# Expert rows two apart, and the experts' products in four column groups, in a two-block transformer with 64 routed experts

## What is computed

```python
# MOE_GROUPS = 8, MOE_PER_GROUP = 8 (64 experts), MOE_TOPK = 2, MOE_FF = 256, D_MODEL = 1024, 512 tokens
g_sel = jnp.argmax(g_logits, axis=-1)
e_prob = jax.nn.softmax(e_logits[tok, g_sel], axis=-1)
top_p, top_i = lax.top_k(e_prob, MOE_TOPK)
gates = g_w[:, None] * top_p / jnp.sum(top_p, axis=-1, keepdims=True)
expert_id = g_sel[:, None] * MOE_PER_GROUP + top_i
...
hid = jax.nn.silu(xb @ w1[e]) * (xb @ w3[e])
return hid @ w2[e]
...
out = jnp.zeros((n_tok + 1, dm), ys.dtype).at[slot_tok].add(ys)[:n_tok]
```

## Time and profile before

| | us |
|---|---|
| median of 3 runs | 1604.18 (1602.31 to 1608.41) |
| the profiled execution, its own time | 1606.86 |
| span of the profile | 1605.1 |
| PE busy in the span | 1407.7 (88%) |
| weight loads PEld | 995.9 (62%) |
| ACT busy | 491.7 (31%) |
| DVE busy | 417.4 (26%) |
| POOL busy | 629.1 (39%) |

### The profile page before, as it was taken

One profiled execution on the slowest core, in us unless ns is written; L12 is line 12 of the kernel. 1 busy time (PEld: TensorE's weight loads), 2 busy tenths in 40 slices (PEclk: granted clock), 3 DMA queues, 4 the chain that ended last, 5 costly groups with the idle time before them and its releaser, 6 DMA issues. The chain is left out here.

```text
span 1605.1 us, 22033 instructions
## 1 busy us (share of the span) xinstructions
PE 1407.7 (88%) x8290; PEld 995.9 (62%) x8290; DVE 417.4 (26%) x1057; ACT 491.7 (31%) x1083; POOL 629.1 (39%) x726
## 2 busy tenths in 40 slices
PE   7999999898999999998999978669988887888781
PEld 6688876676888888886677857434444444444440
DVE  3003047713111102212245041532211111111114
ACT  4326357733322222223464312212211111111111
POOL 4334545443444444443458433123332222222222
PEclk9999999998999999999899989779999999999996
DMA  3322311031332233321313314749999999999964
GB/s 126 119 97 101 109 38 42 29 105 53 105 105 79 79 105 106 105 79 54 118 53 106 105 32 186 301 166 392 393 400 403 407 402 397 391 386 392 389 265 161
DMA packets 91463, 300.17 MB, mean 187 GB/s; under 512 B 12980, under 2 KB 35664, under 8 KB 66816
## 3 DMA queue, kind: packets, MB, share of 16 engines
q1 hardware_dynamic: 83136, 283.37, 47.0%
q0 software_dynamic: 8160, 15.75, 2.8%
q10 hardware_dynamic: 96, 0.08, 0.0%
HBM read 294.94 MB, written 12.62 MB: 192 GB/s over the span
## 5 line engine op out<-in xcount | busy, mean ns | idle before, releaser
L471 POOL TENSOR_TENSOR wring_halves<-wring,wring_halves 128x512 fp32r<-128x512 f32 (+1 forms) x275 | 357.8, 1305 | 409.5 <-ACT wring_halves L466 408.8
L466 ACT CAST wring_halves<-wring 128x512 fp32r<-128x512 f32 (+1 forms) x275 | 168.4, 618 | 465.3 <-PE ps L1035 442.0
L1033 PE MATMUL ps<-wring_halves,big_halves 128*128 128x512 f32 x612 | 244.2, 399 | 16.9 <-POOL wring_halves L471 13.5
L1033 PE MATMUL ps<-hT_halves,wring_halves 128*128 128x512 f32 (+1 forms) x496 | 195.2, 393 | 5.0 <-DVE big_halves L1553 5.0
L1034 PE MATMUL ps<-big_halves,wring_halves 128*128 128x512 f32 (+1 forms) x496 | 194.8, 393 | 0.0
L1035 PE MATMUL ps<-hT_halves,wring_halves 128*128 128x512 f32 (+1 forms) x496 | 194.5, 392 | 0.0
L2209 POOL DMA_INDIRECT y_dram<-xn,sidx x64 | 57.1, 891 | 325.6 <-DVE xn L1969 283.6
L1034 PE MATMUL ps<-wring_halves,hT_halves 128*128 128x512 f32 x436 | 173.1, 397 | 0.0
L1035 PE MATMUL ps<-wring_halves,hT_halves 128*128 128x512 f32 x436 | 172.4, 395 | 0.0
L1460 PE MATMUL ps<-big,arena 128*32 128x256 f32 x1024 | 124.6, 395 | 36.7 <-DMA big<-in_moe_w_dram 36.2
L1033 PEld LDWEIGHTS ps<-wring_halves,big_halves 128*128 128x128 f32 x612 | 117.1, 191 | 45.3 <-POOL wring_halves L471 16.6
(11 more groups left out here) (328 smaller groups left out, 1833.0 us busy)
## 6 DMA issues: line engine op xcount, KB each, us to landing
big<-in_moe_w_dram SPq DMA_DIRECT2D x86, 1024.0 KB, 23.7
wring<-in_moe_w_dram SPq DMA_DIRECT2D x66, 1024.0 KB, 26.3
wring<-in_ffn_w_in_dram SPq DMA_DIRECT2D x22, 1024.0 KB, 6.6
hT<-in_moe_w_dram SPq DMA_DIRECT2D x20, 1024.0 KB, 22.9
wring<-in_fox_w_in_dram SPq DMA_DIRECT2D x7, 2048.0 KB, 8.2
wring<-in_gla_w_in_dram SPq DMA_DIRECT2D x6, 2048.0 KB, 7.9
mkv<-in_moe_w_dram SPq DMA_DIRECT2D x10, 1024.0 KB, 30.1
xn<-in_moe_w_dram SPq DMA_DIRECT2D x10, 1024.0 KB, 30.2
```

The lines of the kernel that those rows point to most:

```text
L466: act.copy(hi, src).then_inc(s_hi, 1)
L471: pool.tensor_tensor(lo, src, hi, ALU.subtract).then_inc(s_lo, 1)
L1033: pe.matmul(out, lhs[1], rhs[0], start=start, stop=False)
```

## The change

There are two parts.

**Places.** The index row `iow` used to hold 0, 1, 2, ..., 31. Now it holds 0, 16, 1, 17, 2, 18, ...: row 2s holds place s and row 2s+1 holds place 16+s. An expert with at most 16 tokens now has them in the even rows 0, 2, 4, ..., where it had them in rows 0 to 15. Gather, scatter and the order of the rows in all products follow the same table. Nothing else in them changes.

**Products.** gate_up makes four products of 128 columns for each k instead of two of 256, each into its own 32 rows of the bank: group i has half i // 2 of the hidden width and its even or odd elements. The gate part is then 128 rows by 64 columns, and so is the up part. The silu and the product take one instruction each instead of two. The two transposes become two ordinary products with the identity, each of 64 columns in its own 64 rows of one bank. expert_down makes four products of 256 columns for each k instead of two of 512. The copies to `ye` are two of 32x256 on each of ACT and DVE instead of one of 32x512.

```diff
-                act.activation(msg[j % 2][0:C, :], bank(2 + j % 2)[0:C, 0:P], ACT.Silu)
-                act.activation(msg[j % 2][G2:G2 + C, :], bank(2 + j % 2)[G2:G2 + C, 0:P], ACT.Silu).then_inc(s_msl, 1)
+                act.activation(msg[j % 2], bank(2 + j % 2)[:, 0:HG], ACT.Silu).then_inc(s_msl, 1)
...
-                act.copy(ye[j % 2][:, 0:512], bank(6 + j % 2)[0:C, :]).then_inc(s_myA, 1)
+                for n in range(2):
+                    last = act.copy(ye[j % 2][:, n * YG:(n + 1) * YG], bank(6 + j % 2)[n * C:(n + 1) * C, 0:YG])
+                last.then_inc(s_myA, 1)
...
                 for k in range(KD):
-                    for q in range(2):
-                        last = pe.matmul(g[q * G2:q * G2 + C, 0:2 * P], xeT[j % 2][:, k, :], w13[:, :, k, :].rearrange("p g (n q) -> p g q n", q=KF)[:, :, q, :],
+                    w = w13[:, :, k, :].rearrange("p g (h n q) -> p g h n q", h=2, q=KF)
+                    for i in range(4):
+                        last = pe.matmul(g[i * C:(i + 1) * C, 0:2 * HG], xeT[j % 2][:, k, :], w[:, :, i // 2, :, i % 2],
                                          start=(k == 0), stop=(k == KD - 1), skip_group_check=True)
...
-                for q in range(2):
-                    r = slice(q * G2, q * G2 + C)
-                    last = pe.transpose(bank(4 + q)[:, 0:C], mhid[j % 2][r, :], ident[r, r])
+                for i in range(2):
+                    r = slice(i * HG, (i + 1) * HG)
+                    last = pe.matmul(bank(4)[r, 0:HG], mhid[j % 2], ident[:, r], start=True, stop=True, skip_group_check=True)
...
-                    for n in range(2):
-                        last = pe.matmul(bank(6 + j % 2)[n * G2:n * G2 + C, :], mhT[j % 2][:, k, :], w2[:, k, n * 512:(n + 1) * 512],
+                    for n in range(4):
+                        last = pe.matmul(bank(6 + j % 2)[n * C:(n + 1) * C, 0:YG], mhT[j % 2][:, k * C:(k + 1) * C], w2[:, k, n * YG:(n + 1) * YG],
                                          start=(k == 0), stop=(k == KF - 1), skip_group_check=True)
...
-                for q in range(2):
-                    r = slice(q * G2, q * G2 + C)
-                    last = dve.tensor_tensor(mhid[j % 2][r, :], msg[j % 2][r, :], bank(2 + j % 2)[r, P:2 * P], ALU.mult)
-                last.then_inc(s_mhid, 1)
+                dve.tensor_tensor(mhid[j % 2], msg[j % 2], bank(2 + j % 2)[:, HG:2 * HG], ALU.mult).then_inc(s_mhid, 1)
...
-            me.inc(pool.iota(iow, pattern=[[1, C]], channel_multiplier=0, **small))
+            me.inc(pool.iota(iow.rearrange("p (s a) -> p s a", a=2), pattern=[[1, C // 2], [C // 2, 2]], channel_multiplier=0, **small))
```

More of the change, by code:

```diff
@@ L77, in program @@
     NB = EXPERTS + SPILL
-    G2 = 64
     assert (META, HD, GK, GV, KF) == (16, 64, 128, 256, 2) and KD == 8 and T == 4
@@ L553, in program @@
         xeT = [arena[:, 4800 + i * KD * C:4800 + (i + 1) * KD * C].rearrange("p (k c) -> p k c", k=KD) for i in range(2)]
[L554 to L558, removed]
+        HG, YG = P // 2, D // 4
+        msg = [arena[:, i * HG:(i + 1) * HG] for i in range(2)]
+        mhid = [arena[:, 256 + i * HG:256 + (i + 1) * HG] for i in range(2)]
+        mhT = [arena[:, 512 + i * 64:512 + i * 64 + KF * C] for i in range(2)]
         arena_at = [640]
@@ L1004, in _ @@
                     act.wait_ge(s_gu, i + (EXPERTS + 1))
-                    act.activation(msg[0][0:C, :], bank(2)[0:C, 0:P], ACT.Silu)
-                    act.activation(msg[0][G2:G2 + C, :], bank(2)[G2:G2 + C, 0:P], ACT.Silu).then_inc(s_msl, 1)
+                    act.activation(msg[0], bank(2)[:, 0:HG], ACT.Silu).then_inc(s_msl, 1)
                     act.wait_ge(s_my, i + (EXPERTS + 1))
                     act.wait_ge(s_ys[0], i * 16 + 8 * EXPERTS)
-                    act.copy(ye[0][:, 0:512], bank(6)[0:C, :]).then_inc(s_myA, 1)
+                    for n in range(2):
+                        last = act.copy(ye[0][:, n * YG:(n + 1) * YG], bank(6)[n * C:(n + 1) * C, 0:YG])
+                    last.then_inc(s_myA, 1)
             for t in range(T):
@@ L1968, in y_out @@
                     dve.wait_ge(s_ys[j % 2], (b - j % 2) * 8)
-                dve.tensor_copy(ye[j % 2][:, 512:1024], bank(6 + j % 2)[G2:G2 + C, :]).then_inc(s_myD, 1)
+                for n in range(2, 4):
+                    last = dve.tensor_copy(ye[j % 2][:, n * YG:(n + 1) * YG], bank(6 + j % 2)[n * C:(n + 1) * C, 0:YG])
+                last.then_inc(s_myD, 1)
             def hT_out(b, j):
@@ L1973, in hT_out @@
                 wait(dve, s_my, b - 1)
-                dve.tensor_copy(mhT[j % 2], hbanks).then_inc(s_mhTe, 1)
+                dve.tensor_copy(mhT[j % 2], bank(4)[:, 0:KF * C]).then_inc(s_mhTe, 1)
             def block_(base, j, first):
@@ L1996, in _ @@
                     dve.wait_ge(s_mhT, i + (EXPERTS + 1))
-                    dve.tensor_copy(mhT[0], hbanks).then_inc(s_mhTe, 1)
+                    dve.tensor_copy(mhT[0], bank(4)[:, 0:KF * C]).then_inc(s_mhTe, 1)
                     dve.wait_ge(s_my, i + (EXPERTS + 1))
                     dve.wait_ge(s_ys[0], i * 16 + 8 * EXPERTS)
-                    dve.tensor_copy(ye[0][:, 512:1024], bank(6)[G2:G2 + C, :]).then_inc(s_myD, 1)
+                    for n in range(2, 4):
+                        last = dve.tensor_copy(ye[0][:, n * YG:(n + 1) * YG], bank(6)[n * C:(n + 1) * C, 0:YG])
+                    last.then_inc(s_myD, 1)
             dve.wait_ge(s_row2, 32)
```

## The result

| | before | with the change |
|---|---|---|
| median of 4 runs each, us | 1605.93 (1602.31 to 1608.41) | 1583.51 (1582.07 to 1585.33) |
| profiled execution, span, us | 1605.1 | 1582.1 |
| mean granted clock | 0.961 | 0.884 |

The ratio is 0.9863, with a 95% interval of 0.9839 to 0.9887, so 22 us less. The forecast was 1585.4 (18.8 us less), with a range of 1578 to 1597.

A forecast was written before the change was run, and what follows sets the result against it. The weights' DMA transfers were taken to set the pace, with PE late only at head and tail. Terms of 12.4 + 4.5 + 0 + 1.9 = 18.8 us less led to 1585.4 us, range 1578 to 1597.

The forecast's parts named there:

- What bounds the kernel: In the experts, the weights' DMA transfers set the pace, 8.47 us per expert; PE is late only at head and tail.
- Two neighbours to an engine: Gathers and scatters: 32 rows shared two neighbours per engine, so 16 tokens burden engines 0 to 7; read from a fit, 8.47.
- Dealt out singly: Rival, 4%: row r goes to engine r mod 16, so even rows lose 12.4 us and the time is 1610.
- the rule of four: Gathers and scatters: four neighbouring rows to an engine would put 16 rows on four engines, pace 9.13 us; argued against.
- The rival of one limit for all: Rival, 10%: the engines share one limit, so how rows are shared is worth nothing; 1597.8 us.
- Term 1: Places, in the stream of weights: even rows take engine 0 from 128 rows each way to 88, saving 12.4 us.
- Term 2: Head, first experts: shorter gate_up and expert_down free slots sooner, so the stream starts in earnest 4.5 us sooner.
- Term 3: Middle of the experts: nothing gained; what PE saves becomes waiting for DMA.
- The sign given for it: Middle: PE busy for about half of 1200 to 1500 us, gate_up near 1.94, granted clock under 1.00 in parts.
- Term 4: Tail, after the last weights land: 3.5 us less at the full clock, 0.3 at 1.2 GHz; the middle, 1.9 us, taken.
- The sum: Whole kernel: 12.4 + 4.5 + 0 + 1.9 = 18.8 us less, forecast 1585.4 us.
- PE as the bound: Rival, 3%: gate_up paced by instruction issue takes 7.7 us, deciding from 6.3 us on; time 1714 us.

The follow-up runs named there:

- Places alone: The kernel before with only the index row of the change; median 1587.54 us, ratio 0.9888 to the kernel before.
- products alone: The changed kernel with the old index row, so tokens in rows 0 to 15; median 1601.98 us, ratio 0.9990 to the kernel before.

## Why the prediction was right, and where it was not

- **What bounds the kernel**: right. A stream whose slowest DMA engine sets the pace, and PE late only at the ends. Places alone and products alone each left the other's part untouched.
- **Two neighbours to an engine**: right as far as tested. Dealt out singly, rows 16 to 31 would lie on the same engines as rows 0 to 15, and two fifths of the gathered rows less would have lowered the pace; it did not. Four neighbours are out by the early and late counts of the first gathers (12 and 4 for 8 rows). The prediction named the rule of four from the Trainium skill, page DMA: Bandwidth & Descriptors, section The descriptor swizzle, and argued against it for these gathers; the trace agrees with the prediction. The argument itself (9.13 against 8.47) was weaker than it looked, since it used the price by bytes that failed; with half the found prices four neighbours would have given 8.45 as well.
- **The rival of one limit for all**: out. The places alone gave 20 us, and with gathers every stretch from 1160 to 1500 us ran at 381 to 411 GB/s in all kernels. That is above the 358 that the Trainium skill's page DMA: Bandwidth & Descriptors, section Where 436 GB/s comes from, gives, so the measurement decides against it here.
- **Term 1, 12.4 us: measured 20.4.** Here a step failed: "0.163 us for 4 KB", the price by bytes at the rate of all engines together. It hit the pace of before (8.48 for 8.47) because two errors met, which was luck. 8 KB pieces were put too high, at 0.326 where the trace's median is 0.313, and gathered rows too low. With 0.34 and 0.14 the kernel before leaves 8.45 - 2 x 0.48 = 7.49 us for its 24 pieces of weights, 0.312 each. Then the streams come out at 57 x 7.49 + 61 x 2 x 0.48 = 485 us before (measured 488), and with 88 / 64 rows at 467 (467.6). 40 / 64 x 0.48 x 61 = 18.3 us is the term as it should have stood; 2 us of the 20.4 stay unexplained. The upper bound of 14.4 failed with the same step, so the range for this term did not hold its value; the range of the whole did.
- **Term 2, 4.5 us: measured 3.75**, in a second profile of the changed kernel 3.6, with products alone 5.2. gate_up at 1.2 GHz and at the full clock was forecast at 3.5 and 1.94 from the product of the meta rows, and took 3.64 and 2.04. Of the two ends, 3.6 and 5.7, it came close to the lower one, because gate_up(1) still ran at 1.2 GHz for most of its time. The first w2 issue (the prediction calls it the second) came at 1072.62 us instead of the 1069.5 forecast; 2.4 us of that come from ahead of the experts.
- **Term 3, nothing**: right. PE is faster at the full clock and its clock falls for it (0.67 to 0.74 from 1160 to 1450 us), as the forecast had it; neither moves the stream. The sign given for it, PE busy for about half of 1200 to 1500 us, did not come: PE was busy for 73 to 75% from 1250 to 1450, since much of its work ran at 1.2 GHz.
- **Term 4, 1.9 us: measured 1.1**, in the second profile 2.0. The last gate_up began at 1.2 GHz (3.64), and the clock rose in expert_down. The forecast for the full clock was 4.8 plus 0.15; kept at the full clock it is 5.3.
- **The sum**: 18.8 forecast; 25.3 for the three terms in this profile, less 2.4 from ahead of the experts; 22 by the medians. The time came within 2 us of the forecast, and that closeness is luck: term 1 was 8 us short, terms 2 and 4 came in 1.6 us smaller together, and the parts ahead of the experts scatter by some us. As a difference, 18.8 us were forecast and the medians moved by 22.4; the forecast counted from 1604.18, and the median of four runs before is 1605.93.
- **PE as the bound**: gate_up was 2.04 us, far from the 6.3 where it would decide.

## What to carry to other kernels

When a stream of large loads sets the pace, ask what each DMA engine carries and not what all carry together: 0.13 MB of token rows beside 3.1 MB of weights cost a whole stage 4% because they sat on half of the engines. Do not trust a price by bytes for small indirect transfers (it held for the scattered row, and the gathered one cost twice as much); take them out or double them once and read the pace. A product made shorter in such a stage buys only its ends, and there at whatever clock the idle time before it has left.

## What the runs showed of the hardware that was not expected

- A 4 KB row that is gathered costs its DMA engine 0.34 us beside a stream of loads, one that is scattered 0.14 (two kernels, four runs). Both kinds of row take 0.160 us in their own packets; the gather's surplus shows in the 8 KB pieces of weights, 8 to 11% of which take over 0.35 us with gathers and none without. The engines together carried 421 GB/s without gathers and at most 411 with them.
- The rows of a gather lie two neighbours to an engine: 8 rows on 4 engines, 15 rows on 8, and with the rows two apart on 8 and 15.
- Four column groups with a moving operand read at a step of two took 2.04 us, against 1.94 for the same number of products read without one (and with 16 stationary columns instead of 32).
- Work of no use kept the clock at 1.00: some 2.9 us of products per expert, where the same kernel without them had 0.66 to 0.80 from 1160 to 1450 us, with PE busy for 67 to 77% of the time.
